# Second mixer's entry of a two-layer hybrid model: last expert group added to transposed rows in PSUM, square sums on TensorE

## The reference, cut to what matters

```python
h = h + hier_moe(rms_norm(h, m_norm[0]), ...)        # experts of layer 0
p = rms_norm(h, o_norm[0]) @ o_w_in[0]               # entry of mixer 2, 3088 columns
h = h + gla_mix(p, ...) @ o_w_out[0]
h = h + hier_moe(rms_norm(h, m_norm[1]), ...)        # experts of layer 1
# expert e: y = y + ((silu(hf @ w_gate[e]) * (hf @ w_up[e])) @ w_down[e]) * combine[:, e:e+1]
```

## Time and profile before

| what | value |
|---|---|
| runs | 851.76 us median of 3 (851.48 to 852.13) |
| the profiled execution: time | 853.37 us |
| the profiled execution: span from first to last instruction | 851.7 us |
| mean granted TensorE clock | 0.977 of full speed |
| TensorE busy | 761.6 us (89%) |
| VectorE busy | 327.3 us (38%) |
| ScalarE busy | 206.2 us (24%) |
| DMA | 242.08 MB, mean 284 GB/s |

### The profile page before, as it was taken

How to read it: one execution, slowest core, us unless ns; L and a number is a source line. 1 busy time by engine, 2 the same in 40 slices (tenths; PEclk the granted TensorE clock), 3 DMA queues, 4 the chain that set the end, 5 groups by cost and what they waited for, 6 DMA issues and landing times.

```text
span 851.7 us, 16959 instructions
## 1 busy us (share of the span) xinstructions
PE 761.6 (89%) x7570; PEld 512.5 (60%) x7570; DVE 327.3 (38%) x689; ACT 206.2 (24%) x419; POOL 12.8 (2%) x62
## 2 busy tenths in 40 slices
PE   8999999899998988899888999999999968766875
PEld 6879777775765546555444878886575544333422
DVE  4566855453336332233335125543242512112213
ACT  3663245421500000000004163452041000000003
POOL 6000000000000000000000000000000000000000
PEclk9999999999999999999999999999999989889888
DMA  8543000506999999999999644003999999999994
GB/s 268 171 116 101 2 3 2 200 2 277 421 416 421 421 419 421 421 411 416 421 403 350 221 126 146 2 2 130 372 387 371 421 422 421 419 421 421 421 412 175
DMA packets 65383, 242.08 MB, mean 284 GB/s; under 512 B 9606, under 2 KB 33276, under 8 KB 42396
## 3 DMA queue, kind: packets, MB, share of 16 engines
q1 hardware_dynamic: 65244, 240.94, 72.0%
q10 hardware_dynamic: 64, 0.02, 0.0%
HBM read 239.90 MB, written 1.05 MB: 283 GB/s over the span
## 4 chain that ended last, share of the span: by engine, by line
PE 75%; DMA 13%; DVE 4%; SPq 3%; issue 2%; ACT 2%; PEldq 0%; POOL 0%; ACTq 0%; DVEq 0%; POOLq 0%
PE ps L1448 11%; PE ps L1211 11%; PE ps L882 10%; PE ps L1166 7%; PE ps L1081 7%; DMA M<-in_m_w_down_dram 5%; PE ps L1250 4%; DMA M<-in_m_w_up_dram 4%; DMA M<-in_m_w_gate_dram 4%; PE ps L1181 4%; SPq L356 3%; PE ps L1033 2%; PE ps L1002 2%; PE ps L838 2%; DVE H L1931 2%
## 5 line engine op out<-in xcount | busy, mean ns | idle before, releaser
L1211 PE MATMUL ps<-M 128*32 128x256 f32 x2016 | 127.0, 404 | 35.0 <-DMA M<-in_m_w_gate_dram 29.2
L1211 PEld LDWEIGHTS ps<-M 128*32 128x32 f32 x2016 | 70.4, 116 | 98.1 <-DMA M<-in_m_w_gate_dram 33.7
L1448 PE MATMUL ps<-M 128*128 128x256 f32 (+2 forms) x400 | 91.2, 385 | 1.0 <-DVE M L1580 1.0
L882 PE MATMUL ps<-M 128*128 128x272 f32 x352 | 88.4, 401 | 1.6 <-DVE M L1580 1.0
L1448 PEld LDWEIGHTS ps<-M 128*128 128x128 f32 (+1 forms) x400 | 73.3, 186 | 15.9 <-issue 3.5
L1166 PE MATMUL ps<-M 128*128 128x128 f32 x688 | 80.3, 276 | 0.0
L1166 PEld LDWEIGHTS ps<-M 128*128 128x128 f32 x688 | 78.3, 192 | 1.8 <-issue 1.8
L882 PEld LDWEIGHTS ps<-M 128*128 128x128 f32 x352 | 64.5, 190 | 16.3 <-issue 2.4
L1928 DVE TENSOR_TENSOR H<-H,ps 128x512 f32<-128x512 f32 x60 | 41.3, 688 | 83.7 <-PE ps L1181 83.5
L1181 PE MATMUL ps<-M 128*128 128x512 f32 x120 | 60.3, 624 | 8.4 <-DVE H L1931 6.0
L1250 PE MATMUL ps<-M 128*32 128x512 f32 x448 | 52.4, 609 | 11.4 <-DMA M<-in_m_w_down_dram 6.7
(11 more groups left out here) (382 smaller groups left out, 856.3 us busy)
## 6 DMA issues: line engine op xcount, KB each, us to landing
M<-in_m_w_gate_dram SPq DMA_DIRECT2D x32, 2048.0 KB, 15.9
M<-in_m_w_up_dram SPq DMA_DIRECT2D x28, 2048.0 KB, 21.7
M<-in_m_w_down_dram SPq DMA_DIRECT2D x28, 2048.0 KB, 22.0
M<-in_o_w_in_dram SPq DMA_DIRECT2D x12, 1024.0 KB, 5.5
M<-in_e_w_in_dram SPq DMA_DIRECT2D x11, 1024.0 KB, 5.4
M<-in_m_w_down_dram SPq DMA_DIRECT2D x9, 1024.0 KB, 20.7
M<-in_m_w_up_dram SPq DMA_DIRECT2D x5, 1024.0 KB, 8.2
M<-in_e_w_out_dram SPq DMA_DIRECT2D x1, 4096.0 KB, 13.9
```

Of the source, the lines that this page charges most:

```text
L882: ins = pe.matmul(ps[:, n % 4, 0:T], wringE[:, (n // 2) % 4, k, (n % 2) * P:(n % 2) * P + P], xnE[:, k], start=(k == 0), stop=(k == KD - 1))
L1211: ins = pe.matmul(ps[32 * e:32 * e + 32, 3 * x, 0:FF], xgT[q % 2][:, k, 32 * e:32 * e + 32], w, start=(k == 0), stop=(k == KD - 1))
L1448: ins = pe.matmul(ps[rows, unit % 4, 0:n], lhs(k), rhs(k), start=(k == 0), stop=(k == KD - 1))
```

## The change

In layer 0 the up unit of q = 7 is loaded and multiplied in two halves, and three of the five combines of group 6 come between them. After the hidden rows of q = 7 are turned, TensorE brings the rows of `H` as they stand then (everything but group 7) into PSUM banks 4 to 7 and 2, transposed, by matmuls with the identity (`old_rows`). When `yst` is there, `new_rows` adds group 7's part to the same PSUM elements, by matmuls of `yst` with the turned routing weights. The combines and additions to `H` stay; two of the additions now stand behind the making of `xnO` in VectorE's list. ScalarE squares the transposed rows in PSUM, and TensorE sums the squares over the partitions by matmuls with a column of ones (`row_sums`, `meta_sums`), then one matmul spreads all 272 factors. VectorE makes `xnO` from PSUM, meta rows apart. The projection's units 0 and 1 run chunk by chunk in turn. The `Sqrt` warm-up of ScalarE moves ahead of the `yst` copy, and `unit_done` of the last down unit now comes after the last `new_rows`. The first mixer's entry does what it did, with other semaphore names. The core of the diff:

```diff
+        RTL = at(27648, T)
+        sqT = [at(b, 512) for b in (29440, 29952, 32640, 33152)]
+        diagO, rsO, xmO, sqm = at(31616, 3, P), at(32000, T), at(32272, KD, META), at(33664, KD, META)
         fnb = H[:, 2, :]
...
                                 sp.dma_start(slots[j][:, :, c0:c0 + 512], down[:, 4 * q:4 * q + 4, c0:c0 + 512]).then_inc(s(f"ld_last{h}"), 16)
+                        elif u == NU - 2 and y == 0:
+                            if h == 0:
+                                sp.dma_start(slots[j][:, :, 0:D], up[:, 4 * q:4 * q + 4, 0:D]).then_inc(s("ld_half"), 16)
+                            else:
+                                for e in (0, 2):
+                                    sp.dma_start(slots[j][:, e:e + 2, D:2 * D], up[:, 4 * q + e:4 * q + e + 2, D:2 * D]) \
+                                        .then_inc(s(f"ld_s{j}"), 16)
...
                     act.wait_ge(s("rt_done"), n + 1)
-                    nc.scalar.activation(RT[q % 2], ps[:, 6, 0:T], ACT.Copy).then_inc(s("rt_set"), 1)
+                    nc.scalar.activation(RTL if q == NQ - 1 and y == 0 else RT[q % 2], ps[:, 6, 0:T], ACT.Copy).then_inc(s("rt_set"), 1)
...
+                        warm_up(ACT.Sqrt)
                     act.wait_ge(s("dn_done"), 2 * n + 1)
-                    nc.scalar.activation(yst[q % 2][:, 0:512], ps[:, 4, :], ACT.Copy).then_inc(s("ya"), 1)
+                    nc.scalar.activation(yst[q % 2][:, 0:512], ps[:, 1 if q == NQ - 1 and y == 0 else 4, :], ACT.Copy) \
+                        .then_inc(s("ya"), 1)
                     if q == 3:
...
+
+            def squared_rows(k):
+
+                act.wait_ge(s("entry_pe"), 3 + k + 2)
+                nc.scalar.activation(sqT[k // 2], ps[:, 4 + k // 2, :], ACT.Square).then_inc(s("entry_act"), 1)
+
+            squared_rows(0)
+            squared_rows(2)
+            act.wait_ge(s("dn_last"), 1)
+            nc.scalar.activation(yst[1][:, 768:D], ps[:, 3, 0:256], ACT.Copy).then_inc(s("yl"), 1)
+            squared_rows(4)
+            squared_rows(6)
+            nc.scalar.activation(sqm, ps[:, 2, 0:P].rearrange("p (k t) -> p k t", k=KD), ACT.Square).then_inc(s("entry_act"), 1)
+            act.wait_ge(s("entry_pe"), 12)
+            nc.scalar.activation(rs[:, 2, 0:2], ps[:, 3, 384:386], ACT.Sqrt, bias=epsb[:, 0:1], scale=1.0 / D)
+            nc.scalar.activation(rs[0:META, 2, 2:3], ps[0:META, 3, 386:387], ACT.Sqrt, bias=epsb[0:META, 0:1], scale=1.0 / D) \
+                .then_inc(s("entry_act"), 1)
+            act.wait_ge(s("entry_pe"), 13)
+            nc.scalar.activation(rsO, ps[:, 0, 0:T], ACT.Copy).then_inc(s("entry_act"), 1)
 
             for n in range(26):
...
+                    if ks[-1] < KD - 1:
+                        return
                     ins.then_inc(s("gate_done" if x == 0 else "up_done"), 1)
...
+                def old_rows(k):
+
+                    at_k = k % 2 * SEQ
+                    for t in range(2):
+                        pe.matmul(ps[:, 4 + k // 2, at_k + t * P:at_k + t * P + P], H[:, t, k * P:(k + 1) * P], ident[:, :],
+                                  start=(k % 2 == 0 and t == 0), stop=False, skip_group_check=True)
+                    pe.matmul(ps[:, 2, META * k:META * k + META], H[:, 2, k * P:(k + 1) * P], ident[:, 0:META],
+                              start=(k == 4), stop=False, skip_group_check=True)
+
+                def new_rows(k):
+
+                    at_k, ys = k % 2 * SEQ, yst[(NQ - 1) % 2][:, k * P:(k + 1) * P]
+                    pe.matmul(ps[:, 4 + k // 2, at_k:at_k + SEQ], ys, RTL[:, META:T], start=False, stop=True, skip_group_check=True)
+                    pe.matmul(ps[:, 2, META * k:META * k + META], ys, RTL[:, 0:META], start=False, stop=True,
+                              skip_group_check=True).then_inc(s("entry_pe"), 1)
+
+                def row_sums(k, n_act):
+
+                    pe.wait_ge(s("entry_act"), 3 + n_act)
+                    for x in range(2):
+                        for t in range(2):
+                            o = x * SEQ + t * P
+                            pe.matmul(ps[:, 3, 384 + t:385 + t], sqT[k // 2][:, o:o + P], ones[:, 0:1], start=(k + x + t == 0),
+                                      stop=(k + x == KD - 1), skip_group_check=True)
+
+                def meta_sums():
+
+                    pe.wait_ge(s("entry_act"), 3 + 5)
+                    for k in range(KD):
+                        ins = pe.matmul(ps[0:META, 3, 386:387], sqm[:, k], ones[:, 0:1], start=False, stop=(k == KD - 1),
+                                        skip_group_check=True)
+                    return ins
...
-                    half_gu(3 * q + 1, q, 1)
+                    if q == NQ - 1 and y == 0:
+                        combined(q - 1, (0, 1))
+                        pe.wait_ge(s("ld_half"), 80)
+                        half_gu(3 * q + 1, q, 1, range(0, 4))
+                        combined(q - 1, range(2, nu))
+                        loaded(3 * q + 1)
+                        half_gu(3 * q + 1, q, 1, range(4, KD))
+                    else:
+                        if q:
+                            combined(q - 1)
+                        loaded(3 * q + 1)
...
                     for k in range(2):
                         ins = pe.transpose(ps[:, 0, FF + k * P:FF + (k + 1) * P], hid[:, k::2], ident[:, :])
                     ins.then_inc(s("ht_done"), 1)
+                    if q == NQ - 1 and y == 0:
+                        pe.wait_ge(s("rt_set"), n + 1)
+                        for k in (4, 5, 6, 7, 0, 1):
+                            old_rows(k)
                     pe.wait_ge(s("hte"), n + 1)
                     u = 3 * q + 2
...
-                rt_, ys = RT[(NQ - 1) % 2], yst[(NQ - 1) % 2]
-
-                def last_down(c0, w, bank):
+                rt_, ys = RT[(NQ - 1) % 2] if y else RTL, yst[(NQ - 1) % 2]
...
-                                            start=(k == 0), stop=(k == 1))
+                                            start=(first and k == 0), stop=(k == 1), skip_group_check=True)
...
+                if y == 0:
+                    pe.wait_ge(s("ld_last0"), 32)
+                    last_down(0, 512, 1).then_inc(s("dn_done"), 1)
+                    for k in (2, 3):
+                        old_rows(k)
+                    pe.wait_ge(s("ya"), n + 1)
+                    for k in range(4):
+                        new_rows(k)
+                    last_combine(0, 0, 0)
+                    last_combine(2, 0, 1)
+                    row_sums(0, 1)
+                    row_sums(2, 2)
+                    pe.wait_ge(s("ld_last1"), 32)
+                    pe.wait_ge(s("acc"), at0 + 1)
+                    last_down(512, 256, 0).then_inc(s("dn_done"), 1)
+                    last_down(768, 256, 3, first=False).then_inc(s("dn_last"), 1)
+                    pe.wait_ge(s("acc"), at0 + 2)
+                    last_combine(1, 0, 1)
+                    pe.wait_ge(s("yd"), n + 1)
+                    new_rows(4)
+                    new_rows(5)
+                    pe.wait_ge(s("yl"), 1)
+                    new_rows(6)
+                    new_rows(7)
+                    pe.wait_ge(s("dn_last"), 1)
+                    pe.sem_inc(s("unit_done"), 1)
+                    row_sums(4, 3)
+                    row_sums(6, 4)
+                    meta_sums().then_inc(s("entry_pe"), 1)
+                    pe.wait_ge(s("acc"), at0 + 3)
+                    last_combine(0, 1, 1)
+                    pe.wait_ge(s("entry_dve"), 3 + 1)
+                    last_combine(2, 1, 2)
+                    pe.wait_ge(s("entry_dve"), 3 + 2)
+                    pe.matmul(ps[:, 0, 0:T], ones[:, :], diagO.rearrange("p t c -> p (t c)")[:, 0:T], start=True, stop=True) \
+                        .then_inc(s("entry_pe"), 1)
+                    last_combine(1, 1, 3)
+                    return
                 pe.wait_ge(s("ld_last0"), 32 * (y + 1))
                 last_down(0, 512, 4).then_inc(s("dn_done"), 1)
                 pe.wait_ge(s("rt_set"), n + 1)
                 pe.wait_ge(s("ya"), n + 1)
                 pe.wait_ge(s("acc"), at0)
-                if y == 0:
-                    last_combine(2, 0, 5)
                 last_combine(0, 0, 6)
                 last_combine(1, 0, 7)
-                pe.wait_ge(s("ld_last1"), 32 * (y + 1))
-                if y == 0:
-                    pe.wait_ge(s("acc"), at0 + 1)
...
+                pe.wait_ge(s("acc"), at0 + 1)
                 last_down(768, 256, 6).then_inc(s("dn_last"), 1)
-                if y == 0:
-                    pe.wait_ge(s("dn_last"), 1)
-                    pe.sem_inc(s("unit_done"), 1)
...
-            row_turn(2, (5,))
-            row_turn(0, (5,))
-            row_turn(1, range(4, KD))
-            spread(1, (2, 0, 1))
             unit = 0
...
             def decayed_rows():
...
 
-            for g in range(len(O_GROUPS)):
+            group_loaded(0)
+            group_loaded(1)
```

(95 more changed lines are left out.)

74 lines of the change are left out of this document (27 added, 47 removed).

## The result

The changed kernel takes 864.24 us (median of 4 runs, 861.84 to 865.15), the kernel before beside it 851.94: a ratio of 1.0135 with a 95% interval of 1.0109 to 1.0162, slower by 12.3 us. I had forecast slower by 7.0, with a range up to 862.0. The direction holds, the size does not, and the measured time lies outside the range. A second set of the same kernel on another occasion gave 863.1 (861.6 to 865.29), beside 852.42 of before.

The account below looks back on a forecast made before the run. TensorE was taken to bound the kernel (75% of the chain, DMA 13%). Halved up unit -1.0, TensorE's work +10.6 and waits -2.6 make +7.0 us on a median of 851.76: 858.8 us, range 856.2 to 862.0.

Parts of the forecast that it names:

- Part 3: TensorE's waits from the hidden rows' turn through projection units 0 and 1: 4.5 us fall to 1.9, so -2.6 us.
- Rival (b): Granted clock falls around the new one-column work; some 3.4 us at half rate adds 3.4, giving 862.2 us; chance 0.06.
- The terms that were counted: The forecast's sum over the halved up unit, TensorE's work and its waits: +7.0 us.
- The first part of the change: Up unit of q = 7 in halves fills TensorE's wait for VectorE's adds of the meta rows: -1.0 us.
- TensorE's added work: New matmuls `old_rows`, `new_rows`, `row_sums` and `meta_sums` add 14.2 us; with 3.6 removed, +10.6 us.
- (a): Small TensorE passes are cheap, 64 at 0.045 us instead of 0.101: 855.2 us, or 854.0 by issue floor; chance 0.07.
- (c): Identity matmuls pass once and narrow ones hide under wide ones on TensorE: -0.5 us, 851.3 us; chance 0.04.
- (d): Group 8 or `o_w_out` loads come too late and unit 9 waits; 2 us of wait gives 860.8; chance 0.02.

Follow-up runs that it names:

- wide sums: The changed kernel with the row sums of squares multiplying 64 columns of ones instead of 1, and the meta rows' 16; 862.21 us.
- full tiles: The wide sums with unit 0's weights 128 columns wide instead of 16, units 0 and 1 still interleaved; 859.75 us.

## Why the prediction was wrong

The distance grew by 12.81 us in the first profile (11.90 in the second). Its parts, each from a pair of kernels: 2.39 clock (changed against wide sums; 1.48 in the second profile), 2.18 width changes in units 0 and 1 (wide sums against full tiles), and the rest, full tiles against before, 42.57 - 34.33 = 8.24. The forecast of +7.0 was a forecast of the last part only; in the timed medians full tiles stand 7.5 us over the kernel before beside them (859.75 and 852.29).

**Part 3 failed in its last sentence, that a chunk of the interleaved units costs TensorE 0.46 + 0.43 us and "their 7.1 us stay": they took 9.5 (8 x 1.19).** I took a chunk pair at the sum of the rates of the earlier trace rows, 0.46 + 0.43. Both rates come from runs of equal weight tiles. Between widths the load does not run under the matmul before, and the pair costs 1.19. The sign was in the trace before, where a combine of the meta rows (16 columns wide, L1317) is followed by one of a token tile (128, L1314). Two weight-load rows of its timeline, which I had not used:

```profile
451.29 0.15 PEld L1317 LDWEIGHTS ps<-M 128*16 128x16 f32 x4 [1.64 <-issue]
...
451.86 0.30 PEld L1314 LDWEIGHTS ps<-M 128*128 128x128 f32 x2 [0.42 <-issue]
```

The load unit sat 0.42 us before the wider tile, with nothing in the profile that it waited for. I priced the combines by their moving columns alone and did not ask what stood between them.

**Rival (b) came true, with the right mechanism and a smaller price, and its chance of 0.06 was the second fault.** It named the suspect (one-column work), the level and +3.4; measured was 2.4 in one profile and 1.5 in the other. The reason that I gave against it, that no wait for a load of 5 us stands here, was no reason. In the earlier trace rows the lower clock followed a wait, in the profiles here it follows one-column matmuls on a TensorE that shows no idle time. (It stands behind other waits for loads of layer 1 as well, with a mean clock of 0.50 from 755 to 760 in the trace before, so my "the rest was at 2.4" holds only for the unit of the earlier trace rows.) The price is less than half of the low stretch (2.39 of some 7 us, 1.48 of some 3.5), because part of the work there waits for ScalarE and VectorE anyway: in the first profile the wait of 0.44 us before the first chunk, which the wide sums show, is gone.

**The terms that were counted**, 8.2 against 7.0. The first part of the change won 0.6 to 0.8, not 1.0: the combine ahead of it takes 1.05 us to the start of the half unit (438.12 to 439.17), not 0.86, and the two halves take 3.8 where the whole took 3.66. `old_rows` took 0.67 to 0.69 each (0.65 forecast), `new_rows` 0.65 (0.63), `row_sums` 0.117 a pass where I took L849's 0.101, and so just above my upper end of 0.113: 3.7 instead of 3.2. `meta_sums` took 0.5, not 0.7. Together TensorE's added work is 14.9 where 14.2 was forecast, which with the first part makes 1.0 of the 1.2; the other 0.2 stays open.

**The other rivals.** (a) is refuted: a one-column pass on 128-column weights costs 0.117 us and a 64-column one 0.119. The Trainium skill ("TensorE: Matmul & The Clock Gate", LDWEIGHTS) gives a weight load as its columns over 1.2 GHz, by an estimate 107 ns for 128 columns. The passes measured here (0.101 to 0.119 us) lie near that load and far from the issue floor of about 25 ns that the prediction took from the same page. (c) is refuted by the two records of each matmul in the trace after. (d) is refuted: the first half of the up unit was there at 439.17, when TensorE began it without a wait for DMA, and `o_w_out`, issued 7.7 us later than before (463.51), held nothing up: TensorE's timeline shows no wait for DMA from unit 2 (484.19) to 529, and unit 9 lies in between.

**Where the expected gain of the design went.** It takes the additions to `H` out of the way to the mixer's input, and it does: two of them run behind `xnO`. But the old order had only 4.5 us of waits there, and the change pays for them with 14.9 us of matmuls against 3.6 removed. Two identity matmuls stand for each pair of transposes at twice the passes, and a full contraction of 128 rows stands for a sum that ScalarE's accumulator had made beside the squares. Without the old rows the kernel was still 6 us slower than before (858.53 against 852.42), and without the sums nearly 10 (861.88 against 852.22).

## What to carry to other kernels

Before moving work to TensorE to save waits of other engines, count passes: with fp32 operands and a new 128-column weight tile each, a pass took 0.101 us with 16 moving columns, 0.117 with 1 and 0.119 with 64, but 0.03 on 16-column tiles (`meta_sums`). The weights set the price, so a "small" sum is not small. Avoid interleaving matmuls whose weight tiles differ in width; if they must be interleaved, pad the narrow one. And where a run of one-column matmuls stands, give them 64 columns: the time is the same, and in these runs the clock stayed up.

## What the runs showed of the hardware that was not expected

The granted clock fell to its lower level while TensorE was busy without a gap, in 3 of 4 profiles with one-column sums, and in none of six with 64 columns at the same pace. It came back while wider matmuls ran. What it is in these matmuls that the clock answers to was not tested beyond one against 64 columns. Whether it falls, and for how long (some 3.5 us in one profile, 7 in another), differs between executions. The changed kernel's times spread over 3.3 us against 0.8 for the wide sums, which fits, but is not shown to come from this: the kernel before spread over 6.2 us in one set (850.41 to 856.63) without such sums.

A change of weight width costs 0.30 us a pair here ((1.19 - 0.89), with one change each way), though from the fourth pair on (475.5) VectorE's input was ready (474.54). The profile names nothing that the load waits for, and why it does not run under the matmul before stays open.
